# Token halves at three norm borders, zero products at the start, and wider additions in the last stage

## The chip, the cores and the metric

The kernel is one program on 1 core of a Trainium2 chip. Its engines run side by side, each with its own instruction stream, and wait for each other by semaphores: PE (TensorE, matrix products), DVE (VectorE), ACT (ScalarE), POOL (GpSimd) and SP, which here only starts DMA transfers. The metric is the device time of one launch in microseconds (us). A profile is one further execution, with a record for each instruction.

## The reference

All is fp32, for one sequence of 512 tokens of width 1024. A first block (chunked attention, gated convolution, feed-forward) is followed by two layers, each a mixer and a convolutional feed-forward:

```python
u = rmsnorm(h, norm_g[layer, 0])
y = mixer(u)                       # layer 0: window attention, layer 1: HGRN2; both with memory attention
h = h + rmsnorm(y, norm_g[layer, 1])
f = conv_ffn(rmsnorm(h, norm_g[layer, 2]), ...)
h = h + rmsnorm(f, norm_g[layer, 3])

def rmsnorm(x, g):
    return x * lax.rsqrt(jnp.mean(x * x, axis=-1, keepdims=True) + 1e-6) * g
```

So at each end of a mixer or feed-forward there is a *border*: the whole output y (all 1024 features of a token) must be there before its norm is, and h with it, and only then does the next product begin.

## The kernel before

**Layout.** Activations lie with 128 features on the partitions and the 512 tokens along the free dimension, in DT = 8 tiles of 128 features. A weight matrix is cut into tiles of 128 x 128, eight of them to a slot of 512 KB. All stages take their slots from one stream of 384 slots, through a ring of 6 buffers: SP loads `w_raw`, POOL splits each slot into a rounded part `w_hi` and the rest `w_lo` (L550, L556). Inputs are split likewise, `h_hi` by ACT and `h_lo` by DVE. A tile is three products of 512 columns: w_hi by h_hi, w_hi by h_lo, w_lo by h_hi (L591, L592, L593).

**Stages.** A stage has output blocks c (128 features, one PSUM bank of eight) and kt input tiles k. Most blocks run k inside c. The first four blocks of a stage behind a border are the *lead*: k outside, four banks inside, so that a new input tile is enough for 12 products. `lead_first` takes k = 0 apart: the eight products with h_hi[0] (L641, L642), then the four with h_lo[0] (L645). `bank_free(st, c)` stands ahead of the first product into a bank and waits for `free` of the block that used it last. Each bank's last user is fixed by `place_accumulators`: the fourth lead bank of the three stages behind a border is the one of block 7, the last, of the stage ahead.

**A border.** There are three in question: a_out to ffn_in0 (kt = 12 in a_out), ffn_out0 to b_in (kt = 22), b_out to ffn_in1 (kt = 12). In the first and third the old stage's last block has 12 tiles, in the second 22. DVE takes each output block to y_all (L1795), ACT squares it (L1280), DVE sums the squares (L1805). `last_block` sums the squares over the partitions by products with ones (L894), three tiles ahead of the end for blocks 0 to 6 and after the end for block 7. ACT takes the root (L1290), DVE the reciprocal (L1768), PE spreads rstd over the partitions by products with the identity (L923) into ps_o. Then DVE, for each tile i: scaled_y (L1773, y times gain times rstd), add to x_res (L1784), and, behind ACT's h_hi (L1295), h_lo (L1739). Fifteen filler products of 128 columns (`turning`, L902) stand between these steps. At the end of add_norm, x_sums adds the squares of x (L1758) for the next norm; its root is applied to outputs of the next stage, so that stage need not wait for it at once. POOL's fifth slot of a stage waits for the second h_ready (`held`). y_all and h_hi are the same memory.

**The start.** SP loads slot 0, x in five parts, slot 1, the constants, and slots 2 to 5. The first stage takes tokens on the partitions (L827 to L829): in each slot (two k) four blocks of 128 tokens by six products. Behind the first block of the third slot PE waits for x_total and sums (L707).

**The last stage** (last0, last1: features 0 to 511 and 512 to 1023, kt = 22, 11 slots each) also has tokens on the partitions: block b, 128 tokens. last1 runs its last four slots block by block. ACT squares with a sum (L1683) and takes the root (L1698), ACT and DVE scale the two halves (L1703, L2145), `last_turn` transposes both halves back (L961, 8 transposes), and `last_add` multiplies by the gain and adds to x_res in eight instructions of 128 columns (L2130). SP stores each half.

## Time and profile before

| | |
|---|---|
| three runs | 2367.55, 2369.21, 2377.30 us (median 2369.21) |
| profiled execution | 2367.43 us, its span 2365.6 us |
| PE busy | 2338.2 us, 99% |
| POOL, DVE, ACT busy | 1620.0, 1177.5, 648.0 us |
| DMA | 214.40 MB, mean 91 GB/s |

The span is from the first to the last record. A busy share is of that span. Products overlap: one of 512 columns is shown with 0.39 us, and the next starts before it ends, so work is counted by the distance of starts. "acc<-h_hi,w_hi" is output and inputs by name; L numbers are lines of the kernel.

### The profile page before, as it was taken

How to read it: one execution, taken by the hardware profiler on the slowest of the kernel's cores; microseconds unless marked ns; L12 is line 12 of the kernel's file. 1: busy time of each engine (PE TensorE's matmuls, PEld its weight loads, DVE VectorE, ACT ScalarE, POOL GpSimd, SP SyncE). 2: the span in 40 equal slices, each digit the busy share in tenths (PEclk: the TensorE clock that was granted, in tenths of full speed). 3: DMA queues.
4: the chain of work that ended last, by engine and by line, in shares of the span. 5: the costliest groups of instructions: out<-in, count | busy, mean ns of one | idle time of the engine just before them, and what ended most of it. 6: DMA issues, size and time to landing. Idle time of an engine off the chain costs nothing.

```text
span 2365.6 us, 31358 instructions
## 1 busy us (share of the span) xinstructions
PE 2338.2 (99%) x11222; PEld 1908.7 (81%) x11222; DVE 1177.5 (50%) x1987; ACT 648.0 (27%) x1248; POOL 1620.0 (68%) x2225
## 2 busy tenths in 40 slices
PE   8999999999999999999999999999999999999998
PEld 6877778888888888777788888887888888888886
DVE  4336654333311324577358553045888875756402
ACT  3223321002201212455221110025667652111011
POOL 8664558777877877657569887763455447988872
PEclk9999999999999999999999999999999999999999
DMA  4233223232333332222222333322222212333332
GB/s 172 89 100 96 81 81 98 95 94 96 98 98 98 94 122 97 80 72 90 73 88 94 96 97 98 98 82 70 72 65 71 71 63 83 96 98 98 98 97 63
DMA packets 63406, 214.40 MB, mean 91 GB/s; under 512 B 6688, under 2 KB 10912, under 8 KB 63136
## 3 DMA queue, kind: packets, MB, share of 16 engines
q1 hardware_dynamic: 60528, 206.55, 27.2%
q10 hardware_dynamic: 2736, 5.96, 0.8%
q8 instruction: 89, 1.46, 0.2%
q14 instruction: 53, 0.43, 0.1%
HBM read 210.38 MB, written 2.10 MB: 90 GB/s over the span
## 4 chain that ended last, share of the span: by engine, by line
PE 49%; DVE 3%; ACT 1%; issue 0%; POOL 0%; DVEq 0%
PE acc L591 12%; PE acc L593 12%; PE acc L592 12%; PE acc L944 1%; PE acc L943 1%; PE acc L945 1%; PE ps_o L776 1%; PE ps_s L1147 1%; PE ps_s L734 1%; PE ps_s L591 1%; PE ps_s L593 1%; PE ps_s L592 1%; PE ps_s L1136 0%; PE ps_o L1206 0%; PE ps_s L944 0%; PE ps_s L943 0%
## 5 line engine op out<-in xcount | busy, mean ns | idle before, releaser
L556 POOL TENSOR_TENSOR w_lo<-w_raw,w_hi 128x256 fp32r<-128x256 f32 (+1 forms) x1532 | 1201.2, 816 | 188.7 <-ACT w_hi L1621 174.9
L550 POOL CAST w_hi<-w_raw 128x512 fp32r<-128x512 f32 x688 | 434.7, 661 | 518.3 <-DMA w_raw<-stream 478.7
L591 PE MATMUL acc<-h_hi,w_hi 128*128 128x512 f32 x1701 | 676.8, 398 | 1.0 <-DVE h_lo L1739 1.0
L593 PE MATMUL acc<-h_hi,w_lo 128*128 128x512 f32 x1701 | 663.4, 390 | 0.0
L592 PE MATMUL acc<-h_lo,w_hi 128*128 128x512 f32 x1701 | 662.4, 389 | 0.0
L591 PEld LDWEIGHTS acc<-h_hi,w_hi 128*128 128x128 f32 x1701 | 320.0, 188 | 68.6 <-issue 2.9
L593 PEld LDWEIGHTS acc<-h_hi,w_lo 128*128 128x128 f32 x1701 | 319.3, 188 | 67.6
L592 PEld LDWEIGHTS acc<-h_lo,w_hi 128*128 128x128 f32 x1701 | 319.8, 188 | 65.2 <-issue 2.2
L1320 ACT ACTIVATE probs<-probs,neg_max 128x256 f32<-128x256 f32 (+5 forms) x160 | 86.9, 547 | 128.3 <-DVE neg_max L1852 128.2
L1817 DVE TENSOR_TENSOR hid_tmp<-acc,rstd_in 128x512 f32<-128x512 f32 x82 | 56.7, 692 | 129.7 <-PE acc L593 127.5
L591 PE MATMUL acc<-u_hi,w_hi 128*128 128x512 f32 x256 | 99.6, 389 | 0.0
L592 PE MATMUL acc<-u_lo,w_hi 128*128 128x512 f32 x256 | 99.6, 389 | 0.0
L593 PE MATMUL acc<-u_hi,w_lo 128*128 128x512 f32 x256 | 99.6, 389 | 0.0
L1476 ACT ACTIVATE ffn_tmp<-ffn_tmp 128x512 f32<-128x512 f32 x44 | 27.9, 634 | 246.5 <-DVE ffn_tmp L2096 246.5
L592 PE MATMUL acc<-o_lo,w_hi 128*128 128x512 f32 x232 | 90.4, 390 | 0.0
L1795 DVE COPY y_all<-acc 128x512 f32<-128x512 f32 x22 | 15.2, 692 | 150.9 <-PE acc L593 129.8
L1868 DVE TENSOR_SCALAR probs<-probs,inv_sum 128x256 f32<-128x256 f32 (+3 forms) x160 | 84.2, 567 | 2.8
L2078 DVE TENSOR_TENSOR x_res<-acc,x_res 128x512 f32<-128x512 f32 x16 | 11.1, 692 | 138.7 <-PE acc L593 138.7
L1458 ACT ACTIVATE u_tmp<-u_tmp 128x512 f32<-128x512 f32 x32 | 20.2, 632 | 210.2 <-DVE u_tmp L2070 210.2
L2070 DVE SCALAR_TENSOR_TENSOR u_tmp<-acc,rstd_in 128x512 f32<-128x512 f32 x31 | 21.4, 692 | 104.7 <-PE acc L593 104.4
L591 PE MATMUL acc<-hid_hi,w_hi 128*128 128x512 f32 x176 | 68.6, 390 | 0.0
L592 PE MATMUL acc<-hid_lo,w_hi 128*128 128x512 f32 x176 | 68.5, 389 | 0.0
(430 smaller groups left out, 3939.4 us busy)
## 6 DMA issues: line engine op xcount, KB each, us to landing
w_raw<-stream SPq DMA_DIRECT2D x384, 512.0 KB, 3.5
toeplitz<-ext_in ACTq DMA_DIRECT2D x16, 256.0 KB, 2.8
out<-x_res SPq DMA_DIRECT2D x8, 256.0 KB, 2.3
x_res<-x_in SPq DMA_DIRECT2D x3, 512.0 KB, 6.7
mem<-mem_in ACTq DMA_DIRECT2D x1, 1024.0 KB, 6.7
consts<-consts_in SPq DMA_DIRECT2D x1, 656.0 KB, 9.4
x_res<-x_in SPq DMA_DIRECT2D x2, 256.0 KB, 4.9
rope<-rope_in ACTq DMA_DIRECT2D x1, 512.0 KB, 7.6
```

The lines of the kernel that those rows point to most:

```text
L550: nc.gpsimd.tensor_copy(hi[:, half], raw[:, half]).then_inc(hi_made, 1)
L556: nc.gpsimd.tensor_tensor(lo[:, part], raw[:, part], f32(hi[:, part]), ALU.subtract).then_inc(low_quarter if not end else split_made if i ...
L591: nc.tensor.matmul(ps, hi, x_hi[:, k, 0:cols], start=(k == 0), stop=False)
L592: nc.tensor.matmul(ps, hi, x_lo[:, k, 0:cols], start=False, stop=False)
L593: mm = nc.tensor.matmul(ps, lo, x_hi[:, k, 0:cols], start=False, stop=(k == st.kt - 1))
L734: nc.tensor.matmul(banks[u.bank][:, u.at:u.at + u.width], u.q, u.k, start=True, stop=True).then_inc(s_ready, 1)
L776: mm = nc.tensor.matmul(ps_o[g[0].out_part:g[0].out_part + rows, g[first].out_cols[0]:g[end - 1].out_cols[1]].rearrange("p (u n) -> p u n" ...
L943: nc.tensor.matmul(out_, hid_hi[:, k, cols], hi, start=(k == 0), stop=False)
L1320: nc.scalar.activation(part, part, ACT.Exp, scale=-1.0, bias=small["neg_max"][:, b:b + 1], accum_out=small["row_sum"][:, b:b + 1]).then_in ...
L1476: nc.scalar.activation(t_, t_, ACT.Gelu_apprx_tanh).then_inc(gelu_ready, 1)
L1817: step(nc.vector.tensor_tensor(dst, src, by, ALU.mult), st.free)
L1868: step(nc.vector.tensor_scalar(part, part, inverse[:, i:i + 1], None, ALU.mult), pn_ready)
```

## The change

**Start.** 24 products of 128 columns of zeros (L905 of the changed kernel) run ahead of the first real one, as soon as the zero column exists. Slot 1 is loaded ahead of the last two parts of x.

**Borders.** The old stage's last block is done in two halves of 256 tokens: half A in its bank, then half B in ps_s1. Sums, root, reciprocal and spread of half A lie between tiles of half B (rstd of half A in ps_o). The lead's first three tiles (SPLIT) are done in halves too: k = 0 of half A, the sums of half B, k = 1 of A, the spread of B (into ps_s1), k = 2 of A, then k = 0 to 2 of B, then k = 3 to 7 whole. DVE and ACT have matching halves; from k = 3 on scaled_y comes in two halves and the rest whole. DVE copies half B's block 7 only behind three half tiles of A, and that copy is the `free` of block 7. The copy of block 6 waits for a semaphore at its own end (y6_made), no longer for the slot. The fillers go.

**Last stage.** The gain becomes rows (gain_row, made by 8 transposes within last0); it is multiplied in with the tokens on the partitions, by DVE for last0 (in place of ACT's copy) and within the scaling for last1. `last_add` is then two additions of 4 x 128 columns. last_turn(b - 1) comes ahead of the last slot of block b.

The core of the diff (where a function is written anew, its new lines alone):

```diff
+        WARM = 24
+        gain_row = ar("gain_row", [2, T], 88)
+        HALVES = (slice(0, T // 2), slice(T // 2, T))
+        SPLIT = 3
...
+                if i == 3:
+                    sp.dma_start(w_raw[:, 1, :], stream[1]).then_inc(loaded[1], 16)
                 sp.dma_start(x_res[:, part, :], x_in[:, part, :]).then_inc(x_loaded[i], 16)
-            sp.dma_start(w_raw[:, 1, :], stream[1]).then_inc(loaded[1], 16)
...
+            def half_lead(st, k, half, border, first):
+                cols = HALVES[half]
+                made, ready, at = (x_hi_made, h_ready, first) if half else (xa_made, ha_ready, SPLIT * border)
+                if k % 2 == 0:
+                    pe.wait_ge(split_made, st.first_slot + k // 2 + 1)
+                pe.wait_ge(made, at + k + 1)
+                s, t = (st.first_slot + k // 2) % RING, BANKS * (k % 2)
                 for c in range(BANKS):
+                    if k == 0 and half == 0:
+                        bank_free(st, c)
+                    ps = banks[st.banks[c]][:, cols]
+                    nc.tensor.matmul(ps, w_hi[:, s, t + c, :], h_hi[:, k, cols], start=(k == 0 and half == 0), stop=False)
+                    nc.tensor.matmul(ps, w_lo[:, s, t + c, :], h_hi[:, k, cols], start=False, stop=False)
+                pe.wait_ge(ready, at + k + 1)
                 for c in range(BANKS):
+                    mm = nc.tensor.matmul(banks[st.banks[c]][:, cols], w_hi[:, s, t + c, :], h_lo[:, k, cols], start=False, stop=False)
+                if half and k % 2:
+                    mm.then_inc(slot_done, 1)
+            def border_lead(st, border):
+                first = n["h"]
+                half_lead(st, 0, 0, border, first)
+                border_sums()
+                half_lead(st, 1, 0, border, first)
+                border_rstd()
+                half_lead(st, 2, 0, border, first)
+                for k in range(SPLIT):
+                    half_lead(st, k, 1, border, first)
+                for k in range(SPLIT, st.kt):
+                    pe.wait_ge(h_ready, first + k + 1)
+                    lead_step(st, k, h_hi, h_lo)
...
+            pe.wait_ge(zero_made, 1)
+            for _ in range(WARM):
+                nc.tensor.matmul(ps_o[:, 0:P], small["zero"][:].to_broadcast([P, P]), small["zero"][:].to_broadcast([P, P]), start=True, stop=True)
...
+            def last_block(st, x_hi, x_lo, sq):
+                tiles = st.kt
+                half_tiles(st, 0, tiles - 3, 0, x_hi, x_lo)
                 n["rms"] += 1
                 n["y"] += 1
+                border.update(st=st, sq=sq[:, (DT - 1) % 2, :])
                 take_t(rms_ready, n["rms"])
                 pe.wait_ge(y_sq_used, (DT - 2) * n["y"])
+                half_zero(0)
+                half_sums(rstd_in, 0, False)
+                half_tiles(st, tiles - 3, tiles, 0, x_hi, x_lo).then_inc(ya_made, 1)
+                pe.wait_ge(s_used, n["unit"])
+                out_free()
+                half_tiles(st, 0, 3, 1, x_hi, x_lo)
+                pe.wait_ge(ya_sq, n["y"])
+                half_sums(border["sq"], 0, True).then_inc(ya_sum, 1)
+                half_tiles(st, 3, 6, 1, x_hi, x_lo)
+                pe.wait_ge(ra_used, n["y"])
+                half_rstd(0, ps_o).then_inc(ya_rstd, 1)
+                half_tiles(st, 6, tiles, 1, x_hi, x_lo)
+            def border_sums():
+                half_zero(1)
+                half_sums(rstd_in, 1, False)
                 pe.wait_ge(y_sq, DT * n["y"])
+                half_sums(border["sq"], 1, True).then_inc(y_sum, 1)
+            def border_rstd():
+                pe.wait_ge(border["st"].free, DT)
                 pe.wait_ge(rms_used, n["rms"])
+                half_rstd(1, ps_s[1]).then_inc(y_rstd, 1)
...
+                    if s in (1, 2):
+                        for i in range(BANKS):
+                            mm = nc.tensor.transpose(ps_s[s - 1][:, i * P:(i + 1) * P],
+                                                     param("norm_g", 56 + BANKS * (s - 1) + i).to_broadcast([P, P]), const("ident"))
+                        mm.then_inc(gain_turned, 1)
...
                 for b in range(BLOCKS):
                     for s in range(st.slots - LAST_SLOTS, st.slots):
+                        if b and s == st.slots - 1:
+                            last_turn(b - 1)
                         last_slot(st, s, [b])
-                    if b:
-                        last_turn(b - 1)
                 last_turn(BLOCKS - 1)
...
+                def first_half(i):
+                    act.wait_ge(xa_ready, SPLIT * (n["y"] - 1) + i + 1)
+                    nc.scalar.activation(h_hi[:, i, HALVES[0]], x_res[:, i, HALVES[0]], ACT.Copy, scale=gain(i)).then_inc(xa_made, 1)
                 n["next"] += 1
+                first_half(0)
+                first_half(1)
+                act.wait_ge(slot_done, st.made(DT - 1))
+                nc.scalar.activation(sq[:, (DT - 1) % 2, HALVES[1]], ps_s[1][:, HALVES[1]], ACT.Square).then_inc(y_sq, 1)
+                first_half(2)
+                act.wait_ge(y_sum, n["y"])
+                nc.scalar.activation(rms[:, 2:4], ps_t[:, 2:4], ACT.Sqrt, scale=1.0 / D, bias=small["eps_d"][:]).then_inc(rms_ready, 1)
+                n["rms"] += 1
                 for i in range(DT):
                     act.wait_ge(x_ready, first + i + 1)
-                    x_half(i, gain)
-                    if summed:
-                        x_square(i, x_squares[:, i, :] if i else ps_t[:])
+                    if i < SPLIT:
+                        nc.scalar.activation(h_hi[:, i, HALVES[1]], x_res[:, i, HALVES[1]], ACT.Copy, scale=gain(i)).then_inc(x_hi_made, 1)
...
+                dve.wait_ge(ra_ready, n["y"])
+                inverse(0, ra_used)
+                dve.wait_ge(ya_rstd, n["y"])
+                scaled_y(0, 0)
+                for i in range(SPLIT):
+                    add(i, 0)
+                    if i + 1 < SPLIT:
+                        scaled_y(i + 1, 0)
+                        rest(i, 0)
+                dve.wait_ge(y_sq, DT * n["y"])
+                step.wait()
+                step(nc.vector.tensor_copy(y_all[:, DT - 1, HALVES[1]], ps_s[1][:, HALVES[1]]), st.free)
+                rest(SPLIT - 1, 0)
                 dve.wait_ge(rms_ready, n["rms"])
+                inverse(1, rms_used)
                 dve.wait_ge(y_rstd, n["y"])
+                scaled_y(0, 1)
+                for i in range(DT):
+                    add(i, 1)
+                    if i + 1 < DT:
+                        if i + 1 >= SPLIT:
+                            scaled_y(i + 1, 0)
+                        scaled_y(i + 1, 1)
+                    rest(i, 1)
...
+                for half in range(2):
+                    tiles = slice(half * BANKS, (half + 1) * BANKS)
+                    dve.wait_ge(last_turned, 2 * b + half + 1)
+                    step.wait()
+                    step(nc.vector.tensor_tensor(x_res[:, tiles, cols], banks[stages["last0"].banks[2 * (b % 2) + half]][:].rearrange("p (i n) -> p i n", n=P),
+                                                 x_res[:, tiles, cols], ALU.add), last_x)
...
+                dve.wait_ge(gain_made, 2)
+                for b in range(BLOCKS):
+                    dve.wait_ge(last_sum, b + 1)
+                    step.wait()
+                    step(nc.vector.tensor_tensor(last_y[:, b, :], banks[stages["last0"].banks[b]][:], gain_row[:, 0, :], ALU.mult), last_taken)
...
-                    if b:
-                        last_add(b - 1)
+                    step(nc.vector.scalar_tensor_tensor(last_o[:, b % 2, 1, :], banks[stages["last1"].banks[b]][:], last_inv[:, b:b + 1],
+                                                        gain_row[:, 1, :], ALU.mult, ALU.mult), last_scaled[1])
+                    if b < BLOCKS - 1:
+                        last_add(b)
                 last_add(BLOCKS - 1)
             def mixer_out(layer):
...
```

PE at the first border, from the end of a_out's last block to the lead of ffn_in0 (consts are ones or the identity, rstd_in the sum of squares of blocks 0 to 6, square that of block 7). Before:

```order
L593 MATMUL acc<-o_hi_114,w_lo 128x512
L902 MATMUL acc<-consts 128x128 [waits free_a_out]
L902 MATMUL acc<-consts 128x128 x3
L894 MATMUL ps_t<-consts,square 128x1 [waits y_sq]
L894 MATMUL ps_t<-consts,square 128x1 x3
L902 MATMUL acc<-consts 128x128 [waits free_a_out]
L902 MATMUL acc<-consts 128x128
L923 MATMUL ps_o<-consts,rstd 128x128 [waits rms_used,o_copied]
L923 MATMUL ps_o<-consts,rstd 128x128 x3
L902 MATMUL acc<-consts 128x128 [waits free_a_out]
L902 MATMUL acc<-consts 128x128 x8
L641 MATMUL acc<-h_hi,w_hi 128x512 [waits free_a_out,x_hi_made,split_made]
```

And now, from half B's last product (L960) to k = 1 of half A:

```order
L960 MATMUL ps_s<-o_hi_114,w_lo 128x256
L663 MATMUL acc<-h_hi,w_hi 128x256 [waits free_a_out,xa_made,split_made]
L664 MATMUL acc<-h_hi,w_lo 128x256
L663 MATMUL acc<-h_hi,w_hi 128x256 [waits free_a_out]
L664 MATMUL acc<-h_hi,w_lo 128x256
L663 MATMUL acc<-h_hi,w_hi 128x256 [waits free_a_out]
L664 MATMUL acc<-h_hi,w_lo 128x256
L663 MATMUL acc<-h_hi,w_hi 128x256 [waits free_a_out]
L664 MATMUL acc<-h_hi,w_lo 128x256
L667 MATMUL acc<-h_lo,w_hi 128x256 [waits ha_ready]
L667 MATMUL acc<-h_lo,w_hi 128x256 x3
L939 MATMUL ps_t<-columns,consts 128x2
```

The fillers are gone, lead products follow the old stage directly, and the sums of half B (L939 and what follows) stand behind the fourth bank's wait for a_out's `free`.

DVE at the same border, from the reciprocal of half A on. Before, the reciprocal is followed by the tiles in turn:

```order
L1768 RECIPROCAL rstd<-rms 128x4 [waits free_a_out,rms_ready]
L1773 SCALAR_TENSOR_TENSOR ps_s<-y_all,params,ps_o 128x512 [waits rms_used,y_rstd]
L1784 TENSOR_TENSOR x_res<-ps_s,x_res 128x512 [waits dve_own]
L1773 SCALAR_TENSOR_TENSOR ps_s<-y_all,params,ps_o 128x512 [waits x_ready]
L1739 SCALAR_TENSOR_TENSOR h_lo<-x_res,params,h_hi 128x512 [waits dve_own,x_hi_made]
```

Now, from the second half tile's end:

```order
L1868 SCALAR_TENSOR_TENSOR ps_s<-y_all,params,ps_o 128x256 [waits xa_ready]
L1889 SCALAR_TENSOR_TENSOR h_lo<-x_res,params,h_hi 128x256 [waits dve_own,xa_made]
L1875 TENSOR_TENSOR x_res<-ps_s,x_res 128x256 [waits ha_ready]
L1909 COPY y_all<-ps_s 128x256 [waits xa_ready,y_sq]
L1889 SCALAR_TENSOR_TENSOR h_lo<-x_res,params,h_hi 128x256 [waits free_a_out,xa_made]
L1896 RECIPROCAL rstd<-rms 128x2 [waits ha_ready,rms_ready]
L1868 SCALAR_TENSOR_TENSOR ps_s<-y_all,params,ps_s 128x256 [waits rms_used,y_rstd]
```

The copy of half B (L1909) stands behind the third half tile's addition, and the whole tiles' work behind a second reciprocal.

PE at the end of last1, from its last product on. Before:

```order
L945 MATMUL ps_t<-w_lo,hid_hi 128x512
L961 MATMUL acc<-consts,y_all 128x128 [waits last_scaled0,last_x]
L961 MATMUL acc<-consts,y_all 128x128 x3
L961 MATMUL acc<-consts,y_all 128x128 [waits last_scaled1,last_x]
L961 MATMUL acc<-consts,y_all 128x128 x3
L961 MATMUL acc<-consts,y_all 128x128 [waits last_scaled0,last_x]
```

Now:

```order
L1021 MATMUL ps_t<-w_lo,hid_hi 128x512
L1037 MATMUL acc<-consts,y_all 128x128 [waits last_scaled0,last_x]
L1037 MATMUL acc<-consts,y_all 128x128 x3
L1037 MATMUL acc<-consts,y_all 128x128 [waits last_scaled1,last_x]
L1037 MATMUL acc<-consts,y_all 128x128 x3
L1019 MATMUL ps_t<-w_hi,hid_hi 128x512 [waits split_made]
```

The transposes of block 2 stand ahead of the last six products of block 3, no longer behind them.

## Rows read from the trace of the kernel before

**Rows 1.** The page, engines' busy time, share of the span, instructions

```profile
PE 2338.2 (99%) x11222; PEld 1908.7 (81%) x11222; DVE 1177.5 (50%) x1987; ACT 648.0 (27%) x1248; POOL 1620.0 (68%) x2225
```

**Rows 2.** PE's waits: line, waited for, total us, times, longest

```profile
PE acc L827 <- POOL w_lo L556: 9.6, 1, 9.6
```

**Rows 3.** Time line, border one: start us, us, engine, line, out<-in, count [idle before]

```profile
1198.65 1.05 PE L902 MATMUL acc<-consts 128*128 128x128 f32 x8
1198.85 0.60 ACT L1280 ACTIVATE square<-acc 128x512 f32<-128x512 f32 x1 [3.65 <-PE acc L593]
...
1199.50 0.97 PEld L894 LDWEIGHTS ps_t<-consts,square 128*128 128x128 f32 x8
...
1201.18 0.97 PEld L923 LDWEIGHTS ps_o<-consts,rstd 128*128 128x128 f32 x8 [0.27 <-issue]
...
1202.07 2.09 PEld L902 LDWEIGHTS acc<-consts 128*128 128x128 f32 x18
...
1202.38 0.76 DVE L1773 SCALAR_TENSOR_TENSOR ps_s<-y_all,params,ps_o 128x512 f32<-128x512 f32 x1 [1.31 <-PE ps_o L923]
```

**Rows 4.** Time line, PE, the lead's second tile at border one

```profile
1207.93 0.50 PE L591 MATMUL acc<-h_hi,w_hi 128*128 128x512 f32 x1 [0.24 <-DVE h_lo L1739]
```

**Rows 5.** Time line, PE, the first block behind that lead

```profile
1227.13 0.39 PE L591 MATMUL ps_s<-h_hi,w_hi 128*128 128x512 f32 x1
```

**Rows 6.** Time line, PE, products of 256 columns, starts 16 apart

```profile
1021.05 0.28 PE L592 MATMUL acc<-mem_lo_first,w_hi 128*128 128x256 f32 x1
...
1022.96 0.28 PE L593 MATMUL acc<-mem_hi,w_lo 128*128 128x256 f32 x1
```

**Rows 7.** Time line, DVE, five tiles of border one and the last h_lo

```profile
1207.91 0.69 DVE L1784 TENSOR_TENSOR x_res<-ps_s,x_res 128x512 f32<-128x512 f32 x1
...
1219.45 0.75 DVE L1739 SCALAR_TENSOR_TENSOR h_lo<-x_res,params,h_hi 128x512 fp32r<-128x512 f32 x1
1220.24 0.69 DVE L1784 TENSOR_TENSOR x_res<-ps_s,x_res 128x512 f32<-128x512 f32 x1
1221.72 1.01 DVE L1739 SCALAR_TENSOR_TENSOR h_lo<-x_res,params,h_hi 128x512 fp32r<-128x512 f32 x1 [0.79 <-ACT h_hi L1295]
```

**Rows 8.** Groups by form: busy us, mean ns | idle before

```profile
L1817 DVE TENSOR_TENSOR mem_k<-acc,rstd_mem 128x256 f32<-128x256 f32 x8 | 3.4, 425 | 4.4 <-PE acc L593 4.0
L2201 DVE SCALAR_TENSOR_TENSOR mem_lo_last<-mem,params,mem_hi 128x256 fp32r<-128x256 f32 x3 | 1.5, 485 | 1.4 <-ACT mem_hi L1521 1.2
L1521 ACT ACTIVATE mem_hi<-mem,params 128x256 fp32r<-128x256 f32 x8 | 4.0, 501 | 0.0
L1295 ACT ACTIVATE h_hi<-x_res,params 128x512 fp32r<-128x512 f32 x39 | 27.6, 721 | 111.3 <-DVE x_res L2078 77.0 <-DVE x_res L1784 34.3
```

**Rows 9.** Time line, PE, border two: first filler, behind the lead, 12 starts on

```profile
1566.46 1.05 PE L902 MATMUL acc<-consts 128*128 128x128 f32 x8
...
1594.93 0.39 PE L591 MATMUL ps_o<-h_hi,w_hi 128*128 128x512 f32 x1
...
1597.65 1.02 PE L707 MATMUL ps_t<-rstd_in,consts 128*128 128x512 f32 x2
```

**Rows 10.** Time line, the start: PE, POOL and DVE

```profile
11.03 0.63 PE L827 MATMUL acc<-w_hi,h_hi 128*128 128x512 f32 x1
...
11.97 1.63 POOL L550 CAST w_hi<-w_raw 128x512 fp32r<-128x512 f32 x2 [2.44 <-DMA w_raw<-stream]
...
14.45 0.40 PE L829 MATMUL acc<-w_lo,h_hi 128*128 128x512 f32 x1
...
22.47 0.69 DVE L1758 TENSOR_TENSOR rstd_in<-ps_t,x_squares 128x512 f32<-128x512 f32 x1
...
24.21 1.02 PE L707 MATMUL ps_t<-rstd_in,consts 128*128 128x512 f32 x2
```

**Rows 11.** Time line, the tail

```profile
2354.17 1.03 PE L961 MATMUL acc<-consts,y_all 128*128 128x128 f32 x8
...
2356.48 1.06 PE L961 MATMUL acc<-consts,y_all 128*128 128x128 f32 x8 [1.28 <-ACT y_all L1703]
2356.54 6.35 DVE L2130 SCALAR_TENSOR_TENSOR x_res<-acc,params,x_res 128x128 f32<-128x128 f32 x16
```

More of the change, by code:

```diff
@@ L655, in lead @@
+            def lead(st, x_hi, x_lo, ready, then=None):
+                for k in range(st.kt):
+                    ready(k)
+                    lead_step(st, k, x_hi, x_lo)
                     if then is not None:
@@ L904, in last_block, with half_zero, half_rstd @@
-            def last_block(st, x_hi, x_lo, sq, then):
-                tiles = st.cbs * st.kt
-                block_tiles(st, tiles - st.kt, tiles - 3, x_hi, x_lo)
+            def half_zero(half):
+                nc.tensor.matmul(ps_t[:, 2 * half:2 * half + 2], const("ones"), small["zero"][:].to_broadcast([P, 2]), start=True, stop=False)
+            def half_rstd(half, bank):
+                for b in (2 * half, 2 * half + 1):
+                    mm = nc.tensor.matmul(bank[:, b * P:(b + 1) * P], rstd[:, b:b + 1].to_broadcast([P, P]), const("ident"), start=True, stop=True)
+                return mm
@@ L921, in last_block @@
+            def border_rstd():
+                pe.wait_ge(border["st"].free, DT)
                 pe.wait_ge(rms_used, n["rms"])
[L922 to L926 removed]
+                half_rstd(1, ps_s[1]).then_inc(y_rstd, 1)
                 n["o"] += 1
+            border = {}
@@ L1766, in add_norm @@
                 dve.wait_ge(rms_ready, n["rms"])
-                step.wait()
-                step(nc.vector.reciprocal(rstd[:, 0:BLOCKS], rms[:, 0:BLOCKS]), rms_used)
+                inverse(1, rms_used)
                 dve.wait_ge(y_rstd, n["y"])
-                def scaled_y(i):
-                    step.wait()
-                    step(nc.vector.scalar_tensor_tensor(ps_s[i % 2][:], y_all[:, i, :], gain(i), ps_o[:], ALU.mult, ALU.mult),
-                         o_taken if i == DT - 1 else None)
```

211 lines of the change are left out of this document (113 added, 98 removed).

## The prediction

> **What bounds the kernel now.** I read the page first, then TensorE's waits, then the time lines of the places that the change touches. The page has PE busy for 2338.2 us of the 2365.6 us span [rows 1]. Most of the rest is one wait of 9.6 us at the start [rows 2] and the tail of the last stage [rows 11]. So the kernel is a nearly unbroken stream of products, and a change can only act on (a) the start, (b) the time around three borders, where work that PE does is not the stage's own, and (c) the tail. The page's busy share hides (b), because the 15 filler products at each border count as busy.
>
> The profiled execution took 2367.43 us for a span of 2365.6 us; the median of the three runs shown is 2369.21 us. I form the sum as a difference and put it on the median.
>
> **Products, wide and halved.** Products of 512 columns start one each 0.227 us (12 starts from 1594.93 to 1597.65 [rows 9]; 84 of them from 1207.93 to 1227.13 [rows 4, 5] give 0.2286 with small waits). Products of 256 columns start each 0.1194 us: 16 starts between 1021.05 and 1022.96 [rows 6]. Two halves cost 0.239, so 0.012 us more than one whole. The last blocks have 36, 66 and 36 whole products (12, 22, 12 tiles by three): 138 x 0.012 = 1.7 us in sum. For this the Trainium skill, page "TensorE: Matmul & The Clock Gate", section "Back-to-back issue gap", has a gap of N/2.4 + 2.5 ns, which as an estimate would be 109 ns for 256 columns and 216 for 512, and 0.3 us instead of 1.7. The rows of 256 columns are of this same kind of product, and I keep 1.7.
>
> **The border before, first and third (12 tiles).** All times are from B, the start of the last block of the old stage. Before, 36 products (8.17) and ten sum entries (1.12) end at 1198.65, so B = 1189.36. Then fillers stand beside a chain: square, sums, root and reciprocal, spread products (rstd times ident into ps_o), DVE from 1202.38 [rows 3]. The first whole-speed tile k = 1 starts at 1207.93 (B + 18.6) [rows 4], and the first block after the lead at 1227.13 (B + 37.8) [rows 5]: the seven tiles after the first take 19.2, 2.74 each. DVE needs only 2.47 per tile in that stretch (12.33 for five tiles from 1207.91 to 1220.24) [rows 7], so PE sets the pace.
>
> **The border after, same place.** Work of 256 columns: a TENSOR_TENSOR from PSUM takes 0.425 [rows 8] where one of 512 takes 0.69 [rows 7], so half the width saves 0.27; scaled_y then takes 0.49 (0.76 [rows 3]), the addition 0.425, h_lo 0.485 (0.75 without GpSimd beside it). ACT's scaled copy takes 0.50 against 0.72 [rows 8], so its square 0.38 (0.60 [rows 3]). A handover takes 0.03 to 0.07 [rows 3].
> - Half A is 27 products and 6 sum entries of 0.12 in front of the last nine: ready at B + 5.2. (The sum of squares is there in time: block 6's copy now waits for that block's own end, so no longer for four tiles of the next.) Square, then 2 sums at 6.6, root and reciprocal (0.71 from the sums' end, 1199.50 + 0.97, to the spread's 1201.18 [rows 3]; with handover 0.8) at 7.4, spread products behind tile 6: DVE starts at 8.3. Meanwhile PE does half B, to E = B + 10.4.
> - DVE does three half tiles: 0.49 + 0.42, then twice 0.54 (the wait for ACT) + 0.49 + 0.42, with gaps 4.1, to 12.4; then the copy of half B's last block, to 12.85. Only this copy makes `a_out.free` reach 8. PE has `bank_free` in front of each bank of the next stage's first tile, and the fourth bank was used by block 7 of a_out: it wants 8. So PE, which comes there at B + 11.1, stands until 12.9. This wait is new; everything of the border's second half is queued behind it.
> - PE then: 2 products, 4 of h_lo, 10 sum entries to 14.9; the 12 half products of k = 1 to 16.45 (root and reciprocal lie beside them); spread products, and DVE starts half B at 17.1, where before it started everything at 13.0.
> - From there DVE makes k = 0, 1, 2 of half B ready at +2.0, +3.5, +5.55 and k = 3 (512 columns wide, with two halved scaled_y, 1.05) at +8.25, so B + 25.4. PE is through its halves at 23.2 and waits 2.2 us. Then five tiles of 2.74: B + 39.15. DVE's period is now 2.47 + 0.26 = 2.73, just PE's own, so nothing is added later.
> - Against B + 37.8: 1.35 us slower. The fillers that go were hidden anyway, and the two lead tiles fewer that wait for DVE (5.5 us) are less than the later start (4.1) and the longer way to the first wide tile (2.8).
> Bounds for this term: 0.5 (ACT and DVE halves at half of the wide ones) to 2.3 (each DVE half step 0.1 dearer).
>
> DVE's h_lo also shows two prices, 0.75 and up to 1.02, once GpSimd works again [rows 7]. The Trainium skill, page "SBUF — State Buffer", on the engine ports, has this as an exclusive lock on a port pair, where an operation of two SBUF inputs waits for a whole GpSimd operation; by that an h_lo could pay up to 0.7 us, and five tiles up to 2.5 us more. The measured periods already have the real mean, and the 2.73 is made from them.
>
> **Second border (22 tiles).** Half B has 16 tiles behind the spread products instead of 6, so DVE's first half is done long before. E = B + 17.6; square 18.2; the copy waits for it, to 18.6; the fourth bank is open at 18.7, a stall of 0.4. Then the same chain: spread at 22.9, k = 3 at 31.2, the end at 45.0. Before it was 1594.93 less B = 1566.46 - 16.1 = 1550.3: 44.6 [rows 9]. The sums behind x_squares end at 47.85, where PE wants them at 47.75: 0.1. In all +0.5. Bounds -0.5 to +1.5.
>
> Three borders: 1.35 x 2 + 0.5 = +3.2, bounds +0.5 to +6.1.
>
> **The start.** PE begins at 9.59 [rows 2] and its first 11 products start each 0.43 us (8 from 11.03 to 14.45 in 3.42), those after them each 0.227 [rows 10]: the lower level of the clock (1.2 GHz) against 2.4, after an idle stretch. (The granted clock reads 1.00 for both, so durations must tell.) 24 products of zeros, 0.22 each at the full and 0.43 at the low level (fillers: 18 entries, 9 products, in 2.09 [rows 3]; twice that at half the clock), start at about 1.0; with the low level for the 4.9 us that the real ones had it, they end at 8.7, before 9.59. So slot 0 is done at 15.05, not 17.3: 2.3 us. Slot 1's split must be there: it ended at 17.0 only because its load landed at 11.97. One MiB goes behind it now, some 2.7 us at the rate of 2.25 MiB between 5.98 (first tile of x) and 11.97, so it lands at 9.3, and POOL, free at 9.53, is done by 14.6. Tiles 4 to 7 of x come 1.3 later and are still in time for ACT. But one block into slot 2 PE waits for `x_total`: the last of DVE's sums ended at 23.16 (22.47 + 0.69), PE used it at 24.21 [rows 10], and would now be there at 21.9. DVE's chain is not changed, or slows a little where POOL now works. So PE waits till 23.2 to 23.8, and of 2.3 us remain 0.4 to 1.0: I take 0.7. Bounds -2.3 to +1.8 (the rival below).
>
> **The last stage.** Added on PE: 8 transposes for gain_row; 8 transposes take 1.03 of which the last one's drain is 0.27, with its own pitch of 0.11: 0.88 [rows 11]. The row product of last0 goes from ACT to DVE, 4 x 0.7 under 60 us of products: nothing. last_turn(2) comes before PE's last slot: +0.88, after waits that are over (4.1 us of slots against 2.3 of root and scaling). Tail from the end of products: before 2354.17 to the span's end 2365.6, 11.4. After: scaled at +2.3 as before, four transposes, first addition from 2.95 to 3.65, second to 4.4 (0.69 each, against 16 additions in 6.35 us [rows 11]), then 2.7 to the end as before (2362.89 to 2365.6): 7.1. So -4.3 + 0.88 + 0.88 = -2.6. Bounds -3.2 to -1.2 (rearranged additions at up to 1.2 each).
>
> **Sum:** +3.2 - 0.7 - 2.6 = -0.1. On 2369.21 this is 2369.1 us.
>
> **Rivals.**
> - The border waits vanish, and PE only has its own work: 144 half products (17.2), 1.8 and 1.9 of sums and spreads, 13.7: 34.6 against 37.8, and 41.7 against 44.6, so -9.3, not +3.2: 2356.6 us. For it: PE really has that work in hand. Against: DVE's 8.25 us to the first wide tile, all from rows. Half of it (about 2363) needs a shorter copy wait only.
> - The clock falls. The fillers go, and PE stands 1.8 and 2.2 us at borders one and three, 0.4 and 2.2 at two. The longest pause with full rate behind it is 1.28 us (8 transposes in 1.06 behind it, 1.03 ahead of it [rows 11]); behind 9.59 us the rate was half. 2.2 lies between. A low stretch as at the start costs 12 x 0.2 = 2.4 us, three of them 7.3: 2376.4 us. It decides from the point at which a pause of 2.2 us is enough.
> - The zeros don't raise the clock, or hold PE beyond 9.59: 24 x 0.43 from 1.0 end at 11.3, +1.7 instead of -0.7: 2371.5 us.
>
> **Numbers.** Forecast 0.62, first rival in full 0.05, in part 0.15, clock 0.10, zeros 0.08. Range 2360 to 2376: the terms' bounds together, without their extremes, with the partial rival and most of the clock one. This kernel's measurement tells 0.5%, 11.8 us, from no change. Faster by more needs the full first rival and a good start as well: 0.04. Slower by more needs the clock and the upper bounds: 0.03. Within: 0.93.
>
> **What would show it.** In the changed profile: a PE wait of about 1.8 us for the copy of y_all at the fourth bank of borders one and three and 0.4 at two; one of 2.2 us for h_lo of k = 3 at each; full-rate products at once at 9.6 us and then a wait of 1.3 to 1.9 us for the last sum of x_squares; two additions of 0.7 us at the end and a tail near 7.1 us. I am wrong if PE reaches the wide tiles without a pause, if products behind pauses start each 0.43 us, or if the wait for x_total is not there.

## The result and the profile after

The changed kernel takes 2375.41 us (median of 20 runs, 2372.99 to 2378.56), the kernel before 2368.36 us (20 runs). The ratio is 1.0026, 95% interval 1.0019 to 1.0033: 7 us slower by the medians (4.5 to 7.8 by the interval), where the forecast was no change (2369.1). Two of the 20 runs of the kernel before took 2377 us, some 9 above the rest, and most of the kernels below have one to three such runs. The profiled execution took 2375.36 us, its span 2373.5, so 7.9 more than the 2365.6 of [rows 1]. That is the time of the rival in which the clock falls (2376.4 us), though only about half of what was missed is that rival's mechanism.

TensorE's waits after the change (in total, times, longest), to be held against [rows 2]:

```profile
engine line waited for: us in total, times, longest us
PE acc L608 <- DVE h_lo L1835: 7.0, 3, 2.3
PE acc L663 <- DVE y_all L1909: 3.9, 3, 1.8
PE acc L1037 <- ACT y_all L1799: 2.1, 1, 2.1
...
PE acc L863 <- POOL w_lo L573: 1.6, 1, 1.6
...
PE ps_t L743 <- DVE rstd_in L1854: 1.2, 1, 1.2
```

The 9.6 us at the start are 1.6, and both waits that the prediction put at the borders are there, at its sizes. They don't explain the result: they were in the sum. The clock was not. Busy times of three stretches that run from a border's B (first product of the old stage's last block) to the first block after the lead, then of three short ones inside (PEclk is the granted clock as a share of 2.4 GHz):

```profile
core 0: us, PE busy (x) PEld busy (x) DVE busy (x) ACT busy (x) POOL busy (x), PEclk, DMA share, GB/s
1188.49:1231.73 43.24, 39.07 (x234) 35.93 (x232) 28.72 (x51) 14.11 (x26) 23.63 (x33) 0.88 0.19 64
1554.95:1601.15 46.20, 43.22 (x293) 38.91 (x292) 29.35 (x49) 14.11 (x26) 29.06 (x42) 1.00 0.25 80
1982.53:2024.35 41.82, 37.52 (x234) 33.24 (x233) 28.56 (x49) 14.11 (x26) 26.44 (x38) 0.96 0.20 66
1204.00:1209.00 5.00, 5.00 (x24) 5.00 (x25) 1.47 (x4) 0.65 (x2) 0.00 (x0) 0.50 0.00 0
1217.00:1220.00 3.00, 3.00 (x9) 2.33 (x9) 2.79 (x5) 1.25 (x2) 3.00 (x5) 0.56 0.00 0
1999.00:2001.00 2.00, 2.00 (x12) 2.00 (x11) 0.42 (x1) 0.00 (x0) 0.00 (x0) 0.50 0.00 0
```

Before, the first two took 37.77 and 44.6 [rows 3, 5, 9], the third by the same marks 37.8. The account of the 7.9 us, from the same marks in both traces: up to the first border -0.87, borders +5.47, +1.6 and +4.0 (11.1 in sum; 3.2 were forecast), last stage -2.3.

TensorE at the first border, around both pauses (a row is start, duration, engine, line, what; in brackets the idle time ahead of it and who ended it). Compare [rows 5]:

```profile
1199.26 0.28 PE L664 MATMUL acc<-h_hi,w_lo 128*128 128x256 f32 x1
1201.38 0.39 PE L663 MATMUL acc<-h_hi,w_hi 128*128 128x256 f32 x1 [1.84 <-DVE y_all L1909]
...
1204.40 0.41 PE L663 MATMUL acc<-h_hi,w_hi 128*128 128x256 f32 x1
1204.62 0.41 PE L664 MATMUL acc<-h_hi,w_lo 128*128 128x256 f32 x1
...
1209.96 0.28 PE L663 MATMUL acc<-h_hi,w_hi 128*128 128x256 f32 x1
1210.08 0.28 PE L664 MATMUL acc<-h_hi,w_lo 128*128 128x256 f32 x1
...
1216.61 0.79 PE L608 MATMUL acc<-h_hi,w_hi 128*128 128x512 f32 x1 [2.32 <-DVE h_lo L1835]
1217.20 0.63 PE L609 MATMUL acc<-h_lo,w_hi 128*128 128x512 f32 x1
1217.62 0.63 PE L610 MATMUL acc<-h_hi,w_lo 128*128 128x512 f32 x1
...
1220.17 0.39 PE L608 MATMUL acc<-h_hi,w_hi 128*128 128x512 f32 x1
1220.39 0.39 PE L609 MATMUL acc<-h_lo,w_hi 128*128 128x512 f32 x1
```

The half products behind the first pause start each 0.213 us instead of 0.12, the whole ones behind the second each 0.43 instead of 0.227: the 1.2 GHz level. Behind the first pause it sets in about a microsecond after the products resume, and it is still there at 1209. In this execution it came behind both pauses of border one, the first of border three, and neither of border two.

DVE at the same border, to be held against [rows 7]:

```profile
1207.63 0.49 DVE L1868 SCALAR_TENSOR_TENSOR ps_s<-y_all,params,ps_s 128x256 f32<-128x256 f32 x1 [3.16 <-PE ps_s L944]
...
1215.36 1.19 DVE L1835 SCALAR_TENSOR_TENSOR h_lo<-x_res,params,h_hi 128x512 fp32r<-128x512 f32 x1
1216.59 0.69 DVE L1875 TENSOR_TENSOR x_res<-ps_s,x_res 128x512 f32<-128x512 f32 x1
...
1218.43 1.22 DVE L1835 SCALAR_TENSOR_TENSOR h_lo<-x_res,params,h_hi 128x512 fp32r<-128x512 f32 x1
1219.68 0.69 DVE L1875 TENSOR_TENSOR x_res<-ps_s,x_res 128x512 f32<-128x512 f32 x1
```

h_lo takes 1.2 us where before it took 0.75 to 1.01, and a tile takes DVE 3.09 us (1216.59 to 1219.68), not 2.73. GpSimd works without a gap in this stretch, but it did so before as well. The fifth busy time is GpSimd's, for 12 us of the wide tiles before, then after:

```profile
1209.00:1221.00 12.00, 12.00 (x54) 9.92 (x53) 11.10 (x15) 5.90 (x11) 12.00 (x16) 1.00 0.29 89
1212.00:1224.00 12.00, 9.68 (x45) 8.09 (x44) 11.13 (x18) 5.15 (x9) 12.00 (x17) 0.86 0.27 87
```

### The profile page after: what moved, and what is told of

The parts are those of the page before. It is cut to its first block, busy times and chain, and to the rows that moved or that the text cites. A ratio compares the mean times of both kernels' runs of the same rounds, so it can differ in the third digit from the quotient of the medians.

```text
span 2373.5 us, 31872 instructions
## 1 busy us (share of the span) xinstructions
PE 2346.2 (99%) x11440; PEld 1923.7 (81%) x11440; DVE 1194.2 (50%) x2015; ACT 651.1 (27%) x1261; POOL 1619.4 (68%) x2225
## 4 chain that ended last, share of the span: by engine, by line
PE 48%; DVE 4%; ACT 1%; issue 0%; POOL 0%; DVEq 0%
PE acc L608 11%; PE acc L610 11%; PE acc L609 11%; PE acc L1021 1%; PE acc L1019 1%; PE acc L1020 1%; DVE ps_s L1868 1%; PE ps_o L812 1%; PE ps_s L1228 1%; PE ps_s L770 1%; DVE x_res L1875 1%; PE ps_s L608 1%; PE ps_s L609 1%; PE ps_s L610 1%; PE ps_s L1217 0%; PE ps_o L1287 0%
## 5 line engine op out<-in xcount | busy, mean ns | idle before, releaser
L608 PE MATMUL acc<-h_hi,w_hi 128*128 128x512 f32 x1677 | 668.9, 399 | 7.4 <-DVE h_lo L1835 7.0
L610 PE MATMUL acc<-h_hi,w_lo 128*128 128x512 f32 x1677 | 654.6, 390 | 0.0
L609 PE MATMUL acc<-h_lo,w_hi 128*128 128x512 f32 x1677 | 653.7, 390 | 0.0
L609 PE MATMUL acc<-o_lo,w_hi 128*128 128x512 f32 x208 | 81.1, 390 | 0.0
L2216 DVE TENSOR_TENSOR x_res<-acc,x_res 128x512 f32<-128x512 f32 x16 | 11.1, 692 | 137.9 <-PE acc L610 137.9
L1560 ACT ACTIVATE hid_hi<-ffn_tmp 128x512 fp32r<-128x512 f32 x44 | 27.9, 633 | 116.9 <-DVE ffn_tmp L2242 116.9
L608 PE MATMUL acc<-hid_hi,w_hi 128*128 128x512 f32 x154 | 59.9, 389 | 0.0
L609 PE MATMUL acc<-hid_lo,w_hi 128*128 128x512 f32 x154 | 59.9, 389 | 0.0
```

What stands on the lines that cost most here:

```text
L608: nc.tensor.matmul(ps, hi, x_hi[:, k, 0:cols], start=(k == 0), stop=False)
L609: nc.tensor.matmul(ps, hi, x_lo[:, k, 0:cols], start=False, stop=False)
L610: mm = nc.tensor.matmul(ps, lo, x_hi[:, k, 0:cols], start=False, stop=(k == st.kt - 1))
L1560: nc.scalar.activation(hid_hi[:, i, :], t_, ACT.Copy).then_inc(hid_hi_made, 1)
```

## The experiments

Every median stands against a kernel before at 2368.05 to 2368.25 us in the same comparisons. The border lengths (B to the first block after the lead, us), read from each kernel's own TensorE timeline:

| kernel | border 1 | border 2 | border 3 | clock at the three | median us |
|---|---|---|---|---|---|
| predicted for the change | 39.15 | 45.0 | 39.15 | 1 | 2369.1 |
| changed | 43.24 | 46.20 | 41.82 | .88 / 1 / .96 | 2375.4 |
| zeros in the pauses | 40.64 | 46.23 | 40.63 | 1 | 2371.8 |
| GpSimd to k = 5 | 41.44 | 44.91 | 40.66 | falls, 1, falls | 2399.6 |
| zeros, GpSimd to k = 3 | 39.76 | 45.36 | 39.75 | 1 | 2369.1 |
| zeros (only ahead of k = 3), bank wait mended | 38.58 | 45.74 | 38.55 | 1 | 2367.1 |
| and one spread | 36.96 | 44.16 | 36.94 | 1 | 2362.4 |
| that without zeros | 38.54 | 45.72 | 37.21 | falls, falls, 1 | 2366.4 |
| all together | 36.48 | 43.65 | 36.45 | 1 | 2360.8 |

**Borders undone.** The changed start and last stage in the kernel before.

> The changed kernel with its start and last stage, but the three borders of the kernel before. From the two profiles: start -0.66 to -0.87, last stage -2.3 against the kernel before. If the loss is all in the borders (both theories, clock and contention): 3.1 us under the kernel before, 2365.2 us, about 10 us under the changed kernel. If instead the zero products or the gain rows disturb a later stage, it is not below the kernel before.

2364.19 us, ratio 0.9978 (0.9964 to 0.9993). The loss is in the borders (11.2 us between this kernel and the changed one, 11.1 by the border lengths); the other two parts gain 4 us, where 3.3 were forecast.

**Last stage alone.** As above, without the zero products and the earlier load.

> The kernel before with the changed last stage alone. The start and last stage together gave -4.1 us against the kernel before (2364.2); by the profiles the start is -0.7 to -0.9 and the last stage -2.3, by the prediction -2.6. Expected 2365.8 us (-2.4). If it is 2364.5 or less, the start gave nothing; if it is 2367 or more, the start gave more than 2.5.

2366.17 us, ratio 0.9992 (0.9983 to 1.0001). By medians the last stage gives 2.0 and so the start 2.0, not 0.7; by profile marks 2.3 and 0.7 to 0.9. The interval reaches from nothing to 4 us and doesn't part the two readings. A single profile's mark at the start is no sharper: the first border's B lies at 1188.4 to 1189.0 in the ten profiled executions with the changed start, and at 1189.1 to 1190.9 in the four with the old one. The split of the 4 us stays open.

**Zeros in the pauses.** Zero products added onto written columns keep TensorE at work:

```diff
+ def zeros(count, st):
+     for _ in range(count):
+         nc.tensor.matmul(banks[st.banks[0]][:, 0:P], zero, zero, start=False, stop=False)
  ...
+ if c == BANKS - 1: zeros((7, 0, 7)[border], st)   # ahead of bank_free
+ zeros(9, st)                                       # ahead of k = 3
```

> The changed kernel with zero products (added onto columns already written, so the sums stay) in the pauses: 7 in front of the fourth bank's wait at borders one and three, 9 in front of the wait for k = 3 at all three. Theory A (the pauses let the clock fall, and the half rate behind them is most of what was missed): granted clock 1.00 at all three borders, border one ends 43.2 -> about 40.2 us after its start, border three 3.97 -> about 2.4 us of loss, border two as it was (its clock never fell); 4 to 5 us under the changed kernel, about 2371 us. Theory B (DVE's h_lo beside GpSimd is the cause, the clock a bystander): within 1 us of the changed kernel, 2375.

2371.8 us, 3.6 under the changed kernel; ten of twelve runs lie within 0.9 us, where the changed kernel's 20 spread over 5.6. The clock is up at all three borders:

```profile
1188.83:1229.47 40.64, 39.57 (x266) 35.31 (x264) 28.57 (x49) 14.10 (x26) 23.93 (x34) 1.00 0.22 69
1552.69:1598.92 46.23, 45.31 (x311) 40.91 (x310) 29.41 (x49) 14.11 (x26) 29.13 (x42) 1.00 0.25 80
1980.41:2021.04 40.63, 39.60 (x266) 35.30 (x264) 28.56 (x49) 14.11 (x26) 26.39 (x38) 1.00 0.21 70
```

43.24 and 41.82 became 40.6; 46.20, where no clock had fallen, stayed. Work that computes nothing gives back 3.8 us. Theory A holds for about half of what was missed; 1.2 to 1.5 us per border over the prediction are left.

**The pause alone, long and short**, in the kernel before: none, or four, of the last nine fillers.

```diff
- turning(then, 9)          (long)        - turning(then, 9)   (short)
                                          + turning(then, 4)
```

> The kernel before with the last nine filler products of each border left out, nothing else. PE then pauses about 2.5 us ahead of the lead, which is not released earlier or later. Theory A: behind that pause the products start each 0.43 us for some microseconds, granted clock 0.5 there, and each border ends 1.5 to 3 us later: 2373 to 2377 us. Rival: a pause of 2.5 us alone doesn't do it (the clock falls only with the halved work around it): same as before, 2368.4 us, the granted clock at 1.00.

> The kernel before with four instead of nine filler products as the last group of each border (none: a pause of 2.38 us, the granted clock 0.5 for 3.4 us behind it at each border, 2.8 us slower). The pause should now be about 1.4 us. If a fall needs the longer pause, the clock stays at 1.00 at all three borders and the time is that of the kernel before, 2368.3 us. If 1.4 us is enough, 2370 to 2371 us and 0.5 behind some of the pauses, as where nine were left out.

Long: 2371.07 us, ratio 1.0013 (0.9998 to 1.0029), nine of twelve runs spread over 2368.6 to 2372.1: less than the 2373 to 2377 that was expected, and by the times alone not clear of no change. The trace is clearer: the pause is 2.4 us at each border, the lower level stands behind each, and from the first filler to the first block after the lead each border takes 29.5 us instead of 28.5. Second border, then its stretch:

```profile
1575.06 0.47 PE L641 MATMUL acc<-h_hi,w_hi 128*128 128x512 f32 x1 [2.37 <-issue]
...
1576.56 0.63 PE L642 MATMUL acc<-h_hi,w_lo 128*128 128x512 f32 x1
```

```profile
1576.00:1580.00 4.00, 4.00 (x12) 3.09 (x12) 3.69 (x6) 2.26 (x4) 1.72 (x3) 0.58 0.00 0
```

Short: pause 1.48 us, 2367.56 us, ten of eleven runs within 0.8 us, ratio 0.9998 (0.9989 to 1.0006), clock up behind all three borders (two are shown). The profiled execution is the eleventh run, 2376.78 us. What it has too much lies between borders two and three, in one DVE instruction that is dealt with in the last section:

```profile
1206.30:1212.00 5.70, 5.45 (x24) 1.00 0.01 3
1574.00:1578.00 4.00, 3.74 (x17) 1.00 0.00 0
```

So the pause does it, with no halves about, at 1.0 us for each fall. The fillers that I had counted as free to drop were what kept the clock up.

**GpSimd held longer.** Its release moved from k = 1 of half B to k = 5.

```diff
- held[stages[name].first_slot + 4] = (h_ready, tiles + 2)
+ held[stages[name].first_slot + 4] = (h_ready, tiles + 6)
```

> The changed kernel with GpSimd held until h_lo of k = 5 at each border instead of k = 1 of half B. Theory A: k = 3's h_lo falls from 1.19 to 0.75 us, the pause ahead of k = 3 from 2.3 to 1.8 us, the half rate behind the first pause stays, the one behind the second may go: 1.3 to 3 us under the changed kernel, about 2373 us. Theory B: DVE's period falls from 3.05 to 2.7 us, all three borders lose 1.1 to 2 us each less, the clock stays: 2370 us. Rival C: GpSimd starts 10 us later and is then late with the slots behind the lead, so PE waits for splits: slower than the changed kernel.

2399.61 us. Both theories missed the total, but the border itself speaks: with GpSimd idle, h_lo takes 0.75 and a tile 2.63 (1216.26 to 1218.89),

```profile
1215.47 0.75 DVE L1835 SCALAR_TENSOR_TENSOR h_lo<-x_res,params,h_hi 128x512 fp32r<-128x512 f32 x1
1216.26 0.69 DVE L1875 TENSOR_TENSOR x_res<-ps_s,x_res 128x512 f32<-128x512 f32 x1
...
1218.10 0.75 DVE L1835 SCALAR_TENSOR_TENSOR h_lo<-x_res,params,h_hi 128x512 fp32r<-128x512 f32 x1
1218.89 0.69 DVE L1875 TENSOR_TENSOR x_res<-ps_s,x_res 128x512 f32<-128x512 f32 x1
```

and border two, with the clock up, takes 44.91: the prediction's 45.0. What the hold broke lies behind: GpSimd then works off its backlog without a gap, and one DVE instruction of 0.55 us stands for 17.22 and ends as GpSimd runs out of work (DVE, then GpSimd, then GpSimd's busy time in that stretch):

```profile
1244.46 17.22 DVE L2230 TENSOR_SCALAR ffn_tmp<-hid_tmp,params 128x512 f32<-128x512 f32 x1
```

```profile
1258.62 2.78 POOL L573 TENSOR_TENSOR w_lo<-w_raw,w_hi 128x256 fp32r<-128x256 f32 x4
1275.24 1.32 POOL L567 CAST w_hi<-w_raw 128x512 fp32r<-128x512 f32 x2 [13.83 <-DMA w_raw<-stream]
```

```profile
1244.46:1261.68 17.22, 16.95 (x27) 0.89 0.24 79
```

TensorE waits 10.95 us for it there. (My rival C had GpSimd late for TensorE, by missing slots; it was DVE that was late.)

**Another form for that instruction**, the same sum as a SCALAR_TENSOR_TENSOR:

```diff
- nc.vector.tensor_scalar(t_, g, w[1], b, ALU.mult, ALU.add)
+ nc.vector.scalar_tensor_tensor(t_, g, w[1], b.to_broadcast([P, T]), ALU.mult, ALU.add)
```

> The changed kernel with GpSimd held until h_lo of k = 5 (2399.6 us), where one TENSOR_SCALAR (hid_tmp times a column plus a column, 0.55 us) took 17.2 and 12.1 us while GpSimd worked through its backlog without a gap. Here that operation is a SCALAR_TENSOR_TENSOR with the second column spread over the row, same result, about 0.75 us. Theory S (this one form of instruction is kept out for as long as GpSimd leaves no gap): the long ones are gone, each of the other form ends within 1.3 us, and the time is 2370 to 2373 us, as the shorter borders give it. Rival T (any DVE instruction would have stood, or the backlog itself costs the time): 2390 us or more.

2400.2 us: theory S fell. The other form stands as long, up to 17.5 us:

```profile
1246.08 12.36 DVE L2230 SCALAR_TENSOR_TENSOR ffn_tmp<-hid_tmp,params 128x512 f32<-128x512 f32 x1
```

**Zeros, GpSimd held until k = 3.** The same line with tiles + 4.

> The kernel with zero products in both pauses (2371.8 us), GpSimd held until h_lo of k = 3 instead of k = 1 of half B, some 4.5 us longer. Theory (h_lo pays 0.3 to 0.45 us whenever GpSimd works beside it): the period of k = 3 and k = 4 is 2.63 and the contention moves to k = 5 to 7, where PE has less to lose; 0.5 to 1 us less per border, 2369 to 2370.5 us. Rival: GpSimd's backlog grows as where it was held until k = 5 of all tiles, and DVE instructions behind the border are delayed by many us: 2380 us or more.

2369.14 us, 2.7 under the zeros alone: 0.9 per border, the upper end of what was expected. k = 3's h_lo takes 0.75 (1.19 before), k = 4's pays 1.30, and no long instruction follows.

**The fourth bank's wait.** Block 7's half B lies in ps_s1; the bank that the next stage wants held half A alone, and DVE copies that one 7 us earlier. The product now waits for that copy, and zeros stand only ahead of k = 3:

```diff
- bank_free(st, c)
+ if c == BANKS - 1: pe.wait_ge(ya_taken, n["y"])    # set by the copy of half A
+ else: bank_free(st, c)
```

> The changed kernel with 9 zero products ahead of k = 3, and the fourth bank's first product waiting only for the copy of half A out of that bank (made 7 us earlier), not for the copy of half B out of ps_s1. Theory: the stall of 1.8 us at borders one and three goes (no pause, so no fill needed there), and with it all that is behind it comes 1.6 to 1.8 us earlier: border one ends 39.0 us after its start instead of 40.75, in sum 3.4 us under the kernel with both fills (2371.8), 2368.4 us. Rival: DVE's second half waits for ACT's square and the root anyway, which come from half B's own end, so that the stall was hidden: 2371.8 us stays.

2367.12 us, 4.7 under the zeros alone (3.4 expected): 2.1 us less at borders one and three, 0.5 at two. The stall was on the path, and it was not a need of the data.

**One spread.** The spread of half B goes to ps_o beside half A's, and scaled_y is one instruction from k = 3 on.

```diff
- half_rstd(1, ps_s[1]).then_inc(y_rstd, 1)
+ half_rstd(1, ps_o).then_inc(y_rstd, 1)
...
- if i + 1 >= SPLIT:
-     scaled_y(i + 1, 0)
```

> As the kernel with the fourth bank's wait shortened, and the spread of half B written into ps_o beside half A's, so that from k = 3 on scaled_y is one instruction of 512 columns (0.76 us) and not two of 256 (0.49 each, 1.02 with the gap). If DVE's period of 3.05 us beside GpSimd sets k = 3 to 7 (theory), the period falls to 2.8 and k = 3 is ready 0.26 us earlier: 0.26 x 4 = 1.0 us per border, 3 us in all under the kernel with the shortened wait alone, about 2365.5 us. If TensorE's own 2.74 us per tile sets it, only the first 0.26: 0.8 us in all.

2362.38 us, 4.7 less (3 expected). TensorE's five wide tiles take 13.73 us, its own 2.74 each (14.8 with the split scaled_y), so from k = 4 on DVE is off the path. For k = 3 it is not: the nine zeros fill the wait to the end, and the kernel without zeros below starts k = 3 at the same B + 23.2.

This run also tells why h_lo had become dearer. Between it and the one before only the spread and the split of scaled_y differ; GpSimd starts again after 13.4 us in both, as in the kernel before the change, and works without a gap in both. The wide h_lo of k = 3 to 6 at border one took 1.18, 1.24, 1.08 and 1.22 us with scaled_y in halves, and take 0.90, 0.75, 0.92 and 0.75 with it whole:

```profile
1211.00:1223.00 12.00, 12.00 (x60) 10.11 (x60) 10.42 (x14) 5.38 (x9) 12.00 (x16) 1.00 0.28 85
```

**The same without zeros.**

> The kernel of the shortened fourth-bank wait and the one spread, without any zero products at the borders. PE then pauses about 2.0 us ahead of k = 3 and nowhere else. Theory A: that pause (between the 1.4 us that left the clock up and the 2.4 us that let it fall in the kernel before) lets the clock fall at some borders, the time spreads over 2362 to 2369 from run to run as the changed kernel's does, median 2364 to 2366 us. Rival: without the stall at the fourth bank the second pause alone does nothing: 2362 us, tight.

2366.36 us, eleven of twelve runs over 2363.9 to 2368.0: 4.0 more. There are pauses of 1.77 us ahead of k = 3, and behind those of borders one and two the lower level:

```profile
1211.59 0.54 PE L609 MATMUL acc<-h_hi,w_hi 128*128 128x512 f32 x1 [1.77 <-DVE h_lo L1844]
1211.93 0.63 PE L610 MATMUL acc<-h_lo,w_hi 128*128 128x512 f32 x1
```

```profile
1580.56:1584.00 3.44, 3.44 (x8) 2.76 (x9) 3.27 (x4) 1.25 (x2) 3.44 (x5) 0.51 0.00 0
2001.15:2005.00 3.85, 3.85 (x16) 2.92 (x17) 3.64 (x5) 1.41 (x3) 3.85 (x6) 1.00 0.00 0
```

**All together**, with six zeros and GpSimd held until k = 3.

> The kernel of the shortened fourth-bank wait and the one spread (2362.4 us) with GpSimd held until h_lo of k = 3, and 6 instead of 9 zero products ahead of k = 3. There PE waits for nothing behind its 9 zero products, and h_lo of k = 3 took 1.2 us beside GpSimd. If DVE's readiness of k = 3 still sets the end of the border, it comes 0.4 us earlier: 1.2 to 2 us less in all, 2360.5 to 2361.2 us, granted clock 1.00. If the zeros no longer wait for anything, and PE's own 2.74 us per tile sets the rest, as much. Rival: GpSimd's backlog or the clock takes it back: 2362.4 or above.

2360.78 us (2360.66 to 2361.17), ratio to the kernel before 0.9965 (0.9953 to 0.9976): 7.3 us under it, 14.6 under the changed kernel. This version beats both. (The h_lo of 1.2 us that the expectation names was of the earlier kernels; in the one-spread kernel it took 0.90. k = 3 came 0.5 us earlier with GpSimd held, and TensorE followed: DVE did set its start.)

```profile
1188.75:1225.23 36.48, 36.12 (x245) 33.18 (x244) 26.57 (x45) 14.08 (x26) 17.71 (x25) 1.00 0.24 77
1548.46:1592.11 43.65, 43.29 (x306) 40.38 (x304) 27.22 (x45) 14.11 (x26) 23.07 (x33) 1.00 0.27 85
1973.80:2010.25 36.45, 36.08 (x246) 33.19 (x244) 26.54 (x45) 14.07 (x26) 20.07 (x29) 1.00 0.24 76
```

## Why the prediction was wrong

- **Start: right in the marks.** First product at 9.81 (1.58 us of waiting) and at full rate at once, then 1.21 us of waiting for the last sum; the products of rstd_in stand at 23.55 for 24.21, -0.66 for -0.7.
- **Last stage: right.** -2.3 for -2.6.
- **The border up to its first pause: right within 0.25 us.** Half products each 0.12; DVE begins half A at B + 8.2 (8.3), TensorE's half B ends at B + 10.2 (10.4), the copy at B + 12.8 (12.85), stall 1.84 (1.8), at border two 0.22 (0.4).
- **"DVE starts half B at B + 17.1": wrong, it was B + 19.1.** The sums, k = 1 and the spread behind the stall ran at the 1.2 GHz level. At border two, without a fall, the step came at B + 22.5 (22.9). I had this as a rival at 0.10, with 2.4 us at each of three borders; it cost 2.6 at border one, where the clock fell twice, 1.2 at border three, where it fell once, and nothing at two. And I had the row that spoke against dropping the fillers: no pause between 1.28 and 9.59 us had been seen, and 1.8 and 2.2 lay in that gap. I gave the unseen stretch to the side I needed. Fault one: a risk that hung on all three borders and on pauses that I had predicted myself was priced as an outsider. Its share is 3.8 us, by the zeros.
- **"k = 3 ready +8.25 behind it" and "DVE's period is now 2.73": wrong, 8.9 and 3.05.** I took the period of before, 2.47, added 0.26 for the split scaled_y, and left h_lo in it at its price from before (0.75 to 1.01): "the measured periods already have the real mean". They had it for another order of instructions. h_lo took 1.08 to 1.25 us in most of the wide tiles, though GpSimd was no busier than before, and with scaled_y whole again it was back at 0.75 to 1.03. The later release of GpSimd (17.8 us idle for 13.5) isn't the reason: with 13.4 and the split, h_lo still took 1.2. TensorE had 0.27 us per tile to spare (2.74 against 2.47), the forecast had used up 0.26 of it, so what h_lo took more was lost. Fault two: a price measured in one order of DVE's instructions was carried to another, with nothing left to cover an error. Its share is 1.5, 1.2 and 1.5 us over the predicted lengths, with the clock held up. With GpSimd held back until k = 5, border two is 44.91 for 45.0.
- The two shares, 3.8 and 4.2, are 8.0; the borders came out 7.9 over the forecast. That the total fell within the stated range, beside the rival's 2376.4, is luck: neither that rival nor the forecast had the second share.
- **The rival of vanishing waits** gave -9.3 us at the borders if they fell away. In the last version TensorE has no bank stall, zeros fill its wait for k = 3, and the borders are 1.3, 1.0 and 1.3 us shorter than before. With these mends the halves do pay, by 3.6 us, though not by 9.3: six zeros, DVE's k = 3 and its own work still stand in between.

On GpSimd and DVE: h_lo reads two tensors from SBUF, and it took 0.75 us with GpSimd idle and anything from 0.75 to 1.36 beside a GpSimd without a gap. The Trainium skill, page "SBUF — State Buffer", section "Who interferes with whom", has an exclusive lock for that case, with the later one blocked until the earlier instruction finishes. These times agree: the most that was added, 0.61, is less than one of GpSimd's longer instructions there, 0.8. The prediction quoted the rule and its 2.5 us per border as an upper bound, and set it aside for a mean of the kernel before; the runs gave 1.2 to 1.5. That the split of scaled_y moves the start of h_lo against GpSimd's instructions, and so its wait, would fit the rule; it is my reading, and only the change of the price is shown. The 17.22 us don't agree with a wait for one instruction: GpSimd finished 27 in that time.

## What to carry to other kernels

Filler products beside a chain are not free time to be harvested: before dropping them, list every pause that their going opens, and count on a fall of the clock for each one that is longer than any behind which it has always stayed up (here 1.48 us at the borders). A wait on a shared "free" counter should be checked against what really lies in the bank: naming the right copy, one spread, a later release of GpSimd and six zeros turned a loss of 7 us into a gain of 7. An instruction's price beside a busy neighbour is not fixed: here the same h_lo beside the same gapless GpSimd took 0.75 or 1.24 us, by the order of DVE's other instructions. A sum that leaves no spare time in such a stretch needs the dearer price as a bound.
